# Folding the pooling matrices into the output projection, and moving half of a row scaling from VectorE to ScalarE

## The reference, cut to what matters

```python
h = rmsnorm(x, g_pre_mix) * (1 + sc1) + sh1
proj = h @ w_in                                   # v_pool | x_conv | B | C
# mixer A, 4 groups g of 128 channels, window w = 2, 4, 8, 16
d[g] = mean_window(v_pool[g]) - v_pool[g]
y[g] = (d[g] @ pool_w[g]) * pool_scale[g]         # 128x128 matrix per group
y_conv = gate_b * causal_dwconv(gate_c * x_conv, conv_w)
mix = concat([y[0], .., y[3], y_conv], -1) @ w_out
x = x + gt1 * rmsnorm(mix, g_post_mix)
# then the gated ConvFFN on x
```

## Time and profile before

| what | us |
|---|---|
| three timed runs | 759.44, 779.73, 779.76 (median 779.73) |
| the profiled execution, its own time | 758.07 |
| span of its slowest core (core 4) | 756.4 |
| spans of the 8 cores | 749.1 to 756.4 |
| PE busy in the span | 693.2 |
| DVE busy | 491.1 |
| ACT busy | 350.0 |

### The profile page before, as it was taken

How to read it: one execution, slowest core, us unless ns; L and a number is a source line. 1 busy time by engine, 2 the same in 40 slices (tenths; PEclk the granted TensorE clock), 3 DMA queues, 4 the chain that set the end, 5 groups by cost and what they waited for, 6 DMA issues and landing times.

```text
span 756.4 us, 11992 instructions; the slowest of 8 cores (749.1 to 756.4 us)
## 1 busy us (share of the span) xinstructions
PE 693.2 (92%) x4032; PEld 333.1 (44%) x4032; DVE 491.1 (65%) x645; ACT 350.0 (46%) x621; POOL 213.1 (28%) x259
## 2 busy tenths in 40 slices
PE   0169889989999999999999999999999999999996
PEld 0134444444544444444444444444444444444443
DVE  0247857777886888996777522248888888833222
ACT  1325825563647787666454321125454454531111
POOL 4101200011100332235544400005667667540000
PEclk9979999999999999999999999999999999999999
DMA  8999995299624798559997422334443434013311
GB/s 152 206 188 243 204 206 99 86 225 166 177 103 151 173 213 185 140 136 186 170 163 133 77 83 112 113 112 88 81 84 58 82 67 76 2 42 125 112 70 56
DMA packets 30552, 97.28 MB, mean 129 GB/s; under 512 B 4480, under 2 KB 4992, under 8 KB 30364
## 3 DMA queue, kind: packets, MB, share of 16 engines
q0 software_dynamic: 17088, 54.06, 41.5%
q1 hardware_dynamic: 13404, 42.47, 16.6%
HBM read 125.28 MB, written 19.07 MB: 191 GB/s over the span
## 4 chain that ended last, share of the span: by engine, by line
PE 75%; DMA 11%; DVE 5%; issue 4%; ACT 3%; POOL 1%; DVEq 0%; ACTq 0%; POOLq 0%
PE ps L797 46%; PE ps L298 21%; PE ps L289 6%; DMA arena<-w_ada 6%; DMA arena<-w_in_p 5%; DVE arena L1190 2%; POOL arena L543 1%; ACT arena L562 1%; ACT arena L716 1%; PE ps L306 1%; DVE arena L763 1%; DVE arena L953 1%; DVE arena L957 0%; DVE arena L1194 0%; ACT arena L1188 0%
## 5 line engine op out<-in xcount | busy, mean ns | idle before, releaser
L797 PE MATMUL ps<-arena 128*128 128x512 bf16 (+1 forms) x2400 | 440.2, 344 | 9.5 <-DMA arena<-w_in_p 5.2
L797 PEld LDWEIGHTS ps<-arena 128*128 128x128 bf16 x2400 | 201.8, 98 | 237.8 <-issue 19.1
L298 PE MATMUL ps<-arena 128*128 128x512 bf16 (+1 forms) x748 | 161.9, 379 | 0.0
L1190 DVE SCALAR_TENSOR_TENSOR arena<-ps,arena 128x1023 f32<-128x1023 f32 x88 | 112.6, 1280 | 39.8 <-ACT arena L1188 39.8
L1204 POOL TENSOR_TENSOR arena<-arena 128x1024 bf16<-128x1024 f32 x44 | 104.0, 2364 | 97.9 <-DVE arena L1194 59.3
L1194 DVE SCALAR_TENSOR_TENSOR arena<-ps,arena 128x1022 f32<-128x1022 f32 x88 | 112.8, 1282 | 9.1
L298 PEld LDWEIGHTS ps<-arena 128*128 128x128 bf16 (+1 forms) x748 | 73.7, 99 | 87.9 <-issue 0.4
L569 DVE RECIPROCAL arena<-arena 128x1 f32<-128x1 f32 (+1 forms) x67 | 10.7, 159 | 139.1 <-ACT arena L564 138.6
L1188 ACT ACTIVATE arena<-ps,arena 128x1024 f32<-128x1024 f32 x88 | 97.6, 1109 | 0.1
L562 ACT ACTIVATE arena<-ps 128x1024 f32<-128x1024 f32 (+1 forms) x33 | 33.7, 1022 | 137.2 <-PE ps L298 119.4
L289 PE MATMUL ps<-arena 128*128 128x512 bf16 (+2 forms) x352 | 76.2, 363 | 4.6 <-DMA arena<-w_ada 3.3
(11 more groups left out here) (89 smaller groups left out, 379.8 us busy)
## 6 DMA issues: line engine op xcount, KB each, us to landing
arena<-w_up POOLq DMA_DIRECT2D x44, 512.0 KB, 6.0
y<-arena SPq DMA_DIRECT2D x32, 512.0 KB, 2.7
arena<-w_ada POOLq DMA_DIRECT2D x24, 512.0 KB, 15.5
arena<-x SPq DMA_DIRECT2D x22, 512.0 KB, 8.2
arena<-y SPq DMA_DIRECT2D x16, 512.0 KB, 3.4
arena<-w_down POOLq DMA_DIRECT2D x11, 512.0 KB, 11.0
arena<-x POOLq DMA_DIRECT2D x10, 512.0 KB, 22.1
arena<-w_in_j POOLq DMA_DIRECT2D x4, 768.0 KB, 39.7
```

The lines of the kernel that those rows point to most:

```text
L298: inst = e.matmul(out_ap, lhs_list[i], rhs_list[i], start=(first and i == 0), stop=(last and i == n - 1))
L797: inst = e.matmul(o_, l_, r_, start=st, stop=sp_)
L1190: K.op("dve", lambda e: e.scalar_tensor_tensor(tv[:, 1:1024], psv[:, 0:1023], fw_of(1, c), tv[:, 1:1024], ALU.mult, ALU.add), reads=rp + [ ...
```

## The change

Three things are changed.

1. `pool_w` is loaded in another layout (the output channel of each group's matrix along the columns is now along the partitions) and as fp32, into a part of `TMP` that is not yet in use. DVE scales it by `pool_scale` into `POOLW` (`_pw`, four instructions of 128 columns).
2. At n = 7, `wfold(g)` multiplies `POOLW[:, g, :]` by the rows of `w_out` that belong to group g: two matmuls of 512 columns into a pair of PSUM banks (0 and 1 for even g, 6 and 7 for odd g), and one ACT copy of 1024 columns back over those rows of `WOUT`. `PW_item` and `PWS_item` go, with their buffers `DB` and `DBS`; `P_item` writes its difference straight into `BY`, and the sample rows into `BYS`. The output projection waits for the four `wfold` copies.
3. For tiles 8 to 15, `h_dve` keeps the reciprocal on DVE, but the row scaling is an ACT instruction (`activation`, `Copy`, with a scale per row).

```diff
+        if 8 <= t < 16:
+            K.op("act", lambda e: e.activation(out=xn[0:rows, :], in_=XT[xi][0:rows, :], func=AF.Copy, scale=STAT[0:rows, ST_RS1, t:t + 1]),
+                 reads=[r_xt[xi], r_stat[ST_RS1][t]], writes=[r_xn])
+        else:
+            K.op("dve", lambda e: e.tensor_scalar(xn[0:rows, :], XT[xi][0:rows, :], STAT[0:rows, ST_RS1, t:t + 1], None, ALU.mult),
+                 reads=[r_xt[xi], r_stat[ST_RS1][t]], writes=[r_xn])
...
-    dma1("pool", flat(POOLW), pw_d, writes=[r_poolw])
+    PWF = TMP[:, 128:128 + 512]
+    r_pwf = R("pwf")
+    dma1("pool", PWF, pw_d, writes=[r_pwf])
...
+    def _pw(e):
+        inst = None
+        for g in range(4):
+            inst = e.tensor_scalar(POOLW[:, g, :], PWF[:, g * 128:(g + 1) * 128], VECS[:, V_PSC + g:V_PSC + g + 1], None, ALU.mult)
+        return inst
+    K.op("dve", _pw, reads=[r_pwf, r_tmp, r_vecs], writes=[r_poolw])
...
-        Dt, rD = DB[g % 2], r_db[g % 2]
+        Dt, rD = BY[c % 3][:, g, :], r_by[c][g]
...
+    def wfold(g):
+        b = 0 if g % 2 == 0 else 6
+        for hb in range(2):
+            op = K.op("pe", mm_group(PS[:, b + hb, :], [POOLW[:, g, :]], [WOUT[:, g, hb * 512:(hb + 1) * 512]]),
+                      reads=[r_poolw, r_wout[0]], writes=[r_ps[b + hb]])
+        K.op("act", lambda e: e.activation(out=WOUT[:, g, :], in_=PS[:, b:b + 2, :].rearrange("p a n -> p (a n)"), func=AF.Copy),
+             reads=[r_ps[b], r_ps[b + 1]], writes=[r_wfold[g]])
...
-                 reads=rr + r_wout, writes=[r_ps[b + hb]])
+                 reads=rr + r_wfold + [r_wout[1]], writes=[r_ps[b + hb]])
...
-        P_item(c, s, samp)
+        last_p = P_item(c, s, samp)
         V_item(c, s, samp)
-        if n >= 1:
-            PW_item((n - 1) // 4, (n - 1) % 4)
-        if n == 9:
-            PWS_item()
+        if n == 7:
+            for g in range(4):
+                wfold(g)
```

More of the change, by code:

```diff
@@ L422, in build_program @@
     ACC = alloc([128, 512], F32)
-    DB = [alloc([128, 512], BF16) for _ in range(2)]
     VS = alloc([128, 4, NS, PB + DS], F32)
@@ L606, in h_dve @@
         rms_recip(rows, ST_RS1, t)
-        K.op("dve", lambda e: e.tensor_scalar(xn[0:rows, :], XT[xi][0:rows, :], STAT[0:rows, ST_RS1, t:t + 1], None, ALU.mult),
-             reads=[r_xt[xi], r_stat[ST_RS1][t]], writes=[r_xn])
+        if 8 <= t < 16:
[4 more added lines that the diff above has]
+                 reads=[r_xt[xi], r_stat[ST_RS1][t]], writes=[r_xn])
         release_xt(xi)
@@ L664, in build_program @@
     r_xc, r_acc, r_xcs, r_accs = R("xc"), R("acc"), R("xcs"), R("accs")
-    r_dbs = [R("dbs%d" % i) for i in range(4)]
-    r_db = [R("db%d" % i) for i in range(2)]
     r_vs = [R("vs%d" % i) for i in range(4)]
@@ L871, in P_item @@
             s3 = srcb.rearrange("p (s r) -> p s r", r=PB + DS)
-            K.op("dve", lambda e: e.scalar_tensor_tensor(DBS[:, g, :].rearrange("p (s r) -> p s r", r=DS), s3[:, :, PB:PB + DS],
+            K.op("dve", lambda e: e.scalar_tensor_tensor(BYS[:, g, :].rearrange("p (s r) -> p s r", r=DS), s3[:, :, PB:PB + DS],
                                                          1.0 / w, v3[:, :, PB:PB + DS], ALU.mult, ALU.subtract),
-                 reads=[rsrc, r_vs[g]], writes=[r_dbs[g]])
+                 reads=[rsrc, r_vs[g]], writes=[r_bys[g]])
         return op
[L877 to L902, removed]
+    r_wfold = [R("wfold%d" % g) for g in range(4)]
+    def wfold(g):
[5 more added lines that the diff above has]
+             reads=[r_ps[b], r_ps[b + 1]], writes=[r_wfold[g]])
     def V_item(c, j, samp):
@@ L1078, in build_program @@
                 h_load(t)
-    last_pw = PW_item(3, 3)
     p1x = ([(HB[i], r_hb[i]) for i in range(2)] + [(HS, [r_hs]), (POOLW, [r_poolw])] +
-           [(ap, [rr]) for aps, rs in ((VB, r_vb), (TT_, r_tt), (TP, r_tp), (QB, r_qb), (DB, r_db), (XN1, r_xn1)) for ap, rr in zip(aps, rs)] +
-           [(XC, [r_xc]), (ACC, [r_acc]), (XCS, [r_xcs]), (ACCS, [r_accs]), (DBS, r_dbs), (VS, r_vs), (QS, r_qs)])
+           [(ap, [rr]) for aps, rs in ((VB, r_vb), (TT_, r_tt), (TP, r_tp), (QB, r_qb), (XN1, r_xn1)) for ap, rr in zip(aps, rs)] +
+           [(XC, [r_xc]), (ACC, [r_acc]), (XCS, [r_xcs]), (ACCS, [r_accs]), (VS, r_vs), (QS, r_qs)])
     for rr in [r for c in (2, 3) for r in r_h2[c]] + [r_h2s, r_gt]:
@@ L1094, in state_out @@
     def state_out():
[L1095 to L1096 removed]
+        out_ops.append(dma1("sp", nps_d, VS.rearrange("p a b c -> p (a b c)"), reads=r_vs, deps=[last_p]))
+        out_ops.append(dma1("sp", ncs_d, QS.rearrange("p a b c -> p (a b c)"), reads=r_qs, deps=[last_p]))
         out_ops.append(dma1("sp", npc_d, flat(NPC), reads=r_npc))
@@ L1442 @@
         "w_ada2": np.ascontiguousarray(f(w_ada)[0][:, 2 * D:].reshape(2, 4, 128, 16, 256).transpose(3, 0, 2, 1, 4).reshape(16 * 256, 1024)),
-        "w_in_p": pmaj(w_in_[:, 0:512], 512), "w_in_j": pmaj(w_in_[:, 512:], 384), "pool_w": pmaj(f(pool_w)[0].reshape(512, 128), 128),
+        "w_in_p": pmaj(w_in_[:, 0:512], 512), "w_in_j": pmaj(w_in_[:, 512:], 384), "pool_w": np.ascontiguousarray(f(pool_w)[0].transpose(2, 0, 1).reshape(128, 512)),
         "w_out": f(w_out)[0], "w_up": pmaj(w_up_, 256), "w_down": pmaj(f(ffn_w_down)[0], D),
```

3 lines of the change are left out of this document (1 added, 2 removed).

## The result

The changed kernel takes 1.0056 of the time of the kernel before, with a 95% interval of 1.0037 to 1.0075 (17 executions of each). On the profiled execution's own 758.07 us that is 762.3 us (760.9 to 763.8). I had forecast 756.6, a ratio of 0.998: a small gain, and it is a small loss. The plain medians are 777.58 and 760.76 us, because in 13 of 17 executions after, and 4 of 17 before, some cores ran at a lower clock for a long stretch: the ratio leaves these out, so that it rests on four executions after, and the rows of after are those of core 5, which was not among such cores in its execution (span 756.6 us; core 5 of before has 752.8).

What follows compares the result with a forecast made beforehand. The loop was taken as bound by PE in order and two DMA-paced points, hardly by DVE or ACT. Matmuls −0.56 and the line 882 wait −0.9 gave −1.46 us, from 758.07 to 756.6; range 749 to 770.

Steps and rivals of the forecast that it cites:

- Line 882 and the wait for it: In the loop, PE's wait for the eviction of a pooling product goes with the pooling products: −0.9 us.
- its scaling on DVE: Scaling of pool_w, at most 3.0 us, hidden in DVE's idle time before 51.40, after the load lands at 47.3.
- 0.56 for the matmuls: PE's chain, sixteen pooling products out, eight fold matmuls in: +0.74 us up to 153, −1.30 after 170, sum −0.56.
- the 1.051 of the row: Cost in us per row scaling on ACT, taken from squares of 1024 columns from SBUF; eight make 8.4 us.
- Gate pieces 2 and 3 wait for fold 2: In the loop, these gate pieces depend on fold 2; named within the fold's waits, which were taken as 0.
- Waits that the fold adds: Folds sharing PSUM banks wait for copies: 4.1 us if serial, taken as 0 because the planner fills with projections.
- The 5 before 105 are lost: Five pooling products removed before 105 us win nothing; PE reaches the gate piece 1.08 us earlier and waits for w_ada.
- longer by about 1 us: Sign of a right forecast: both w_ada waits remain, the first longer by about 1 us.
- The late output tiles: Rival: shared banks 6 and 7 start the first output tile 12.8 us later; up to 769.4 us; chance 0.18.
- ACT standing in its line: Rival: scaling on ACT waits for DVE's reciprocal, holding evictions, 2.6 us a tile; 767.0, 774.1 at worst; chance 0.10.
- The shorter second stall: Rival: lighter DVE lets w_ada be requested earlier, saving 3.02 us waiting and 1.78 slow clock; 751.8 us; chance 0.12.

Runs made afterwards that it cites:

- The fold alone: The changed kernel without the moved scaling (all row scalings stay on DVE), against the kernel before: 0.9968 [0.9929, 1.0007].
- the last pair of runs: All the change's work, fold's lists, 16 useless matmuls, st_ffn load ahead of second-gate broadcasts, against the kernel before: eight scalings on ACT 0.9956, on DVE 0.9961.
- the run of the kernel before with st_ffn moved: The kernel before with only the st_ffn load issued ahead of the second gate's broadcasts on SP's queue, against the kernel before: 0.9965 [0.9938, 0.9992].
- the fold's lists with the scaling on ACT: The changed kernel's work planned with scalings on DVE, then the eight put into ACT's list, against the kernel before: 1.0027 [0.9989, 1.0064].

## Why the prediction was wrong

**What held.** Line 882 and the wait for it are gone. `pool_w` lands 40.5 us after its issue and its scaling on DVE takes 0.87 us at 47.01, in DVE's idle time. The work on PE's chain fell by about 2.8 us up to 250 us; I had counted 0.56 for the matmuls and left out 1.3 more as waited for anyway, 1.9 together, and a difference of 0.9 is less than such sums tell. The fold alone came out at 0.9968 [0.9929, 1.0007], where my sum has 0.998. The blocks from 343.79 on are as long as before. The eight scalings took 1.137 us each,

```profile
L606 ACT ACTIVATE arena<-arena 128x1024 bf16<-128x1024 f32 x8 | 8.9, 1137 | 0.0
```

not the 1.051 of the row I had taken. The estimate that I had from the Trainium skill, "ScalarE: Activation LUTs", section "What ACT_TABLE_LOAD costs", was 1.132, and this case's trace agrees with it. It decides nothing: 0.7 us on an engine that is busy 46% of the time. The factor of up to three between the engines that the prediction quotes is 1.5 for this scaling of fp32 rows (1137 against 758 ns). One reading was wrong: line 882 was not all of ACT that PE waited for in the loop; before, it waits 1.56 us for line 934 at 92.19 too.

**The step that failed: "Gate pieces 2 and 3 wait for fold 2", at no price, in a list that I took as unchanged.** Under "Waits that the fold adds" I saw that dependence and took 0, since PE would fill with projections. PE did fill. But the gate does not end on PE: its pieces go through DVE, to DRAM and back as a broadcast, 19.2 us from PE's start of piece 2 at 130.19 to line 945 at 149.36, and line 945 must run before the second output tile gets its banks. Before, the pieces led the first output tile by 11.0 us (115.70 and 126.70), now by 9.4. Nor is the time left that I had counted on to make good a late tile: before, the first two tiles are 12.3 us apart and line 953 frees the banks 9.0 us after a tile starts; now PE has only 7.5 us to do between them (139.60 to the start of the wait, 147.06), and line 945 is through after 11.0 (150.64). And the round trip now runs against the two loads of w_ada that pieces 2 and 3 release themselves: POOL issues them at 131.84 and 132.71, 2.9 us ahead of the write to `scr`, where before they were issued at 117.29 and 118.16, 6.8 us ahead of it, with 6.6 us from issue to landing. The load of x at 131.67, 4.0 us ahead of the write on every core, is the third. By the share of the DMA engines that is how a write of 2.0 us came to take 5.4; no run moved these loads alone. PE waits for the round trip, 2.8 us of idle time and 1.5 of low clock on the mean.

But the dependence by itself did not make the kernel slower: the fold alone has it too. What the runs show is that it costs with the list that the scaling brings about. PE is idle for 1.1 to 1.9 us from 120 to 160 in the seven kernels with the fold's list and the gate pieces behind the folds, against 2.6 to 3.1 in the four with the changed kernel's list and its loads in their order (with the low clock, of which some lies near 120 us behind a wait at the first fold, 1.6 to 3.0 and 3.7 to 6.0). That the moved scaling changes PE's list I did not price at all; I had only named a changed order as what would make the whole wrong. With that list the time is 1.0056 and 1.0065, with the scaling on ACT and on DVE. With 16 useless matmuls in both kernels it is 1.0044 with that list and 0.9951 with the fold's, and the intervals do not meet; the scaling is on ACT in the first of these and on DVE in the second, which by the last pair of runs makes no difference.

**The step that was half right: "The 5 before 105 are lost".** They are: idle time from 60 to 120 us is 7.8 before and 7.7 after. But I had said myself that a stall costs more than its length, and counted the first stall as "longer by about 1 us" with no price for the clock. Its length came out near that, 3.5 for 3.1 us on the mean over the cores (5.93 for 3.4 on core 5), while the small waits ahead of it closed. The clock loss went from 0.9 to 3.5 us, and here the 0.9 is at the low end, since the run of the kernel before with st_ffn moved has 2.0. What this is worth in the end is less: taking it away brought 0.12% in the changed kernel (1.0044 against 1.0056, inside the intervals); in that run evictions and the bank of a gate piece were what PE waited for next.

**The rivals.** The late output tiles came true in their first half: the first output tile starts 12.9 us later on core 5, 12.7 on the mean over the cores, and I had worked out 12.8. That the figures agree so well is luck: on core 4, for which I had worked it out, it is 9.1 (136.62 less 127.53), and on core 5 the last reader of the sample item (now line 931) ends at 133.69 and not at 137.44, and the two rounds of fold and copy behind it, with projections listed between them, take 5.9 us and not 2.9. The price was wrong, since PE did not run out of projections at the end of the loop (idle from 260 to 345 us 6.1, before 5.8) but met the late gate at the second tile. ACT standing in its line did not come true, as far as the last pair of runs shows. The shorter second stall did not pay either: 160 to 190 us has 1.2 us of idle time on the mean instead of 1.7, and 1.1 of low clock instead of 0.5.

**What stays open.** How the 6.5 us divide between the two stalls cannot be had by adding repairs: removing either one moved most of the time to the next wait, and the intervals are 0.3% wide on each side. The fold alone and the fold's lists with the scaling on ACT (0.9968 and 1.0027) differ by more than the last pair of runs would have it; the intervals overlap, the second has the stall for st_ffn on four cores of its profile, and whether that is all I do not know.

## What to carry to other kernels

A dependence that PE can fill with other work need not be free: follow what is computed behind it to its last consumer, through DRAM and back if it goes there, and look which loads the same step releases, since these are what it will share the DMA engines with. Where a planner orders the lists, an edit has two effects, the work and the order, and they can be told apart on the chip by keeping the lists and moving the work. Time won in front of a transfer can be lost there twice: on half of the cores here the small waits ahead of it became one of 4 to 6 us, with a spell of low clock behind it.

## What the runs showed of the hardware

The granted clock behind one wait of 5.93 us was 0.50 for 8 us, where before it had been 0.57 on the mean of 4 us behind waits of 0.77 and 2.59 us; core 5, after and before (stretch, length, busy time of PE, PEld, DVE, ACT and POOL, granted clock, DMA share, GB/s):

```profile
101.00:105.00 4.00, 3.50 (x24) 2.57 (x24) 1.42 (x3) 0.58 (x1) 0.70 (x1) 0.50 0.95 270
105.00:109.00 4.00, 3.17 (x15) 1.36 (x14) 3.09 (x9) 3.34 (x8) 0.00 (x0) 0.50 1.03 191
109.00:113.00 4.00, 4.00 (x28) 1.88 (x26) 1.99 (x3) 2.43 (x7) 0.00 (x0) 0.80 0.07 14
```

```profile
105.00:109.00 4.00, 4.00 (x23) 1.75 (x21) 0.83 (x2) 0.00 (x0) 0.71 (x1) 0.57 1.07 167
109.00:113.00 4.00, 4.00 (x43) 2.46 (x41) 0.69 (x1) 2.99 (x5) 0.00 (x0) 1.00 0.66 112
```

About the same idle time in 60 to 120 us (7.8 and 7.7 us) lost 0.9 us to the clock before and 3.5 after. That the longer wait is the reason is not shown: on cores 2 and 4 of after the waits for w_ada are 2.2 us, and 3.4 and 1.7 us are lost, while on cores 2 and 6 of before nothing is lost behind waits of 2.7 and 2.9. But 3.5 us of matmuls without any use (16 of 512 columns) in the middle of the wait kept the clock at 2.4 GHz (granted clock 1.00 from 95 to 120 us on core 5 of the fold alone with 16), and the six kernels with such matmuls lost 0.0 to 0.9 us from 60 to 120, on the mean over the cores, the others with the fold 1.7 to 4.3.
